# One transfer per expert: gate, up and down weights side by side in a diffusion trunk with 64 experts

## What is computed

```
def run_block(args):
    e, tok, wt = args
    xb = t_pad[tok]                                        # the tokens of expert e
    hb = jax.nn.silu(xb @ w_gate[e]) * (xb @ w_up[e])      # (tokens, 256)
    return (hb @ w_down[e]) * wt[:, None].astype(t.dtype)  # (tokens, 1024)
```

## Time and profile before

| | us |
|---|---|
| median of 3 runs (3128.2 to 3129.74) | 3129.06 |
| span of the profiled execution | 3130.5 |
| PE busy with matmuls | 2604.7 (83%) |
| PE weight loads | 1531.1 (49%) |
| DVE / ACT / POOL busy | 843.2 / 615.6 / 539.8 |
| hardware queue, share of 16 engines | 48.1%, 558.02 MB |
| software queue, share of 16 engines | 3.0%, 31.52 MB |

### The profile page before, as it was taken

The page is one execution under the profiler, slowest core; times in us unless marked ns, Lnnn a source line. Parts: engine busy times, 40 slices in busy tenths (PEclk is TensorE's granted clock), DMA queues, the critical chain, the costliest instruction groups (busy, mean ns, idle before and its releaser), DMA issues. The chain is left out here.

```text
span 3130.5 us, 33956 instructions
## 1 busy us (share of the span) xinstructions
PE 2604.7 (83%) x12570; PEld 1531.1 (49%) x12570; DVE 843.2 (27%) x1610; ACT 615.6 (20%) x1211; POOL 539.8 (17%) x502
## 2 busy tenths in 40 slices
PE   5998987889999996888888649789999878888882
PEld 1444556545556544555445334554544445455551
DVE  2443228144200035111111141714300241111113
ACT  2333210124300011111111122004300111111111
POOL 0000002036300001222222120105500022122222
PEclk8968998989999997999999879899999989999996
DMA  9564111002021323999999542101033369999992
GB/s 316 217 234 163 68 34 74 18 6 52 1 61 40 118 110 131 389 396 392 386 381 377 217 148 81 61 18 43 15 81 99 128 269 391 385 380 381 383 395 111
DMA packets 206864, 590.73 MB, mean 189 GB/s; under 512 B 47464, under 2 KB 104851, under 8 KB 156468
## 3 DMA queue, kind: packets, MB, share of 16 engines
q1 hardware_dynamic: 183828, 558.02, 48.1%
q0 software_dynamic: 22944, 31.52, 3.0%
HBM read 584.06 MB, written 51.51 MB: 203 GB/s over the span
## 5 line engine op out<-in xcount | busy, mean ns | idle before, releaser
L1920 PE MATMUL ps<-wgu,moe_xt 128*64 128x256 f32 x4096 | 508.9, 404 | 164.9 <-DMA wd<-in_w_down_e 162.6
L1920 PEld LDWEIGHTS ps<-wgu,moe_xt 128*64 128x64 f32 x4096 | 340.2, 145 | 291.6 <-issue 183.1
L1502 PE MATMUL ps<-u,w_merge 128*128 128x512 f32 (+1 forms) x768 | 282.0, 525 | 3.7 <-DVEq L1519 3.7
L2007 POOL DMA_INDIRECT rows_out<-moe_y,table x128 | 118.3, 924 | 818.5 <-DVE moe_y L2066 797.4
L1928 PE MATMUL ps<-wd,moe_ht 128*64 128x512 f32 x1024 | 247.8, 605 | 1.5 <-DVE moe_ht L2108 1.5
L2102 DVE TENSOR_TENSOR moe_h<-ps,moe_sg 64x256 f32<-64x256 f32 x128 | 54.5, 426 | 628.8 <-ACT moe_sg L2085 628.8
L812 PE MATMUL ps<-u,w_hy 128*128 128x512 f32 (+1 forms) x576 | 209.4, 521 | 5.8 <-PEq L125 5.8
L1502 PEld LDWEIGHTS ps<-u,w_merge 128*128 128x128 f32 x768 | 146.8, 191 | 134.9 <-issue 123.8
L2085 ACT ACTIVATE moe_sg<-ps 64x256 f32<-64x256 f32 x128 | 48.2, 376 | 638.5 <-PE ps L1920 638.5
L1259 POOL TENSOR_SCALAR attn_p<-attn_p,attn_rs 128x768 f32<-128x768 f32 (+1 forms) x80 | 155.1, 1947 | 81.6 <-DVE attn_rs L1428 81.2
L2066 DVE COPY moe_y<-ps 64x512 f32<-64x512 f32 x128 | 88.7, 693 | 265.4 <-PE ps L1928 265.4
(11 more groups left out here) (313 smaller groups left out, 3090.4 us busy)
## 6 DMA issues: line engine op xcount, KB each, us to landing
wgu<-in_w_gate_e SPq DMA_DIRECT2D x128, 1024.0 KB, 7.9
wgu<-in_w_up_e SPq DMA_DIRECT2D x128, 1024.0 KB, 10.6
wd<-in_w_down_e SPq DMA_DIRECT2D x128, 1024.0 KB, 17.6
prep_w<-in_w_ada SPq DMA_DIRECT2D x24, 2048.0 KB, 15.0
w_merge<-in_w_in SPq DMA_DIRECT2D x32, 512.0 KB, 5.3
w_hy<-in_w_in SPq DMA_DIRECT2D x6, 2048.0 KB, 9.5
transfer<-prep_out POOLq DMA_DIRECT2D x10, 1024.0 KB, 6.8
h<-transfer SPq DMA_DIRECT2D x4, 2048.0 KB, 11.4
```

The costliest lines, as they stand in the source:

```text
L1502: last = nc.tensor.matmul(m.ps[:, bank, 0:n], w[:, b, w_at + c], z[:, c, at:at + n], start=c == 0, stop=c == kn - 1)
L1920: last = nc.tensor.matmul(ps[k * SLOTS:(k + 1) * SLOTS, 0:DE], xt[:, c], wgu[:, k, c], start=c == 0, stop=c == KC - 1)
L2007: nc.gpsimd.indirect_dma_start(out=dram["y"], out_offset=bass.IndirectOffsetOnAxis(ap=m.table[0:SLOTS, j:j + 1], axis=0), in_=y[:, j % 2], ...
```

## The change

The three weight arrays of an expert are laid side by side on the host: a new input `w_experts` of (2, 64, 128, 6144), in which each partition's row holds its 2048 numbers of gate, of up and of down, 24 KB in one piece. A ring slot is one tensor of 128 x 24 KB, with views for the gate and up part and for the down part. `load_expert` issues one DMA of 3 MB and 16 is added once to the semaphore, so PE waits for 16 per use in place of 48. The overflow stage is changed in the same way. The order on every engine, the ring of four and the moments at which a slot is refilled are as before.

```diff
-def load_expert(eng, a, l, e, wgu, wd, sem):
-
-    for k, name in enumerate(("w_gate_e", "w_up_e")):
-        eng.dma_start(wgu[:, k], a[name][l, bass.ds(e, 1)].rearrange("o (p c) n -> p (o c) n", p=P)).then_inc(sem, 16)
-    eng.dma_start(wd, a["w_down_e"][l, bass.ds(e, 1)].rearrange("o (p c) n -> p (o c) n", p=P)).then_inc(sem, 16)
+def load_expert(eng, a, l, e, w, sem):
+
+    eng.dma_start(w, a["w_experts"][l, bass.ds(e, 1)].rearrange("o p n -> p (o n)")).then_inc(sem, 16)
+
+
+GU = 2 * KC * DE
+
+
+def gate_up_part(w):
+
+    return w[:, 0:GU].rearrange("p (k c n) -> p k c n", k=2, c=KC)
+
+
+def down_part(w):
+
+    return w[:, GU:GU + 2 * D].rearrange("p (c n) -> p c n", c=2)
...
-    wgu, wd, loaded = ring
+    slots, loaded = ring
+    wgu, wd = [gate_up_part(w) for w in slots], [down_part(w) for w in slots]
...
-                    load_expert(sp, a, l, j, wgu[b], wd[b][:], loaded[b])
+                    load_expert(sp, a, l, j, slots[b][:], loaded[b])
...
-                wait(pe, loaded[b], r * 48 + 48)
+                wait(pe, loaded[b], r * 16 + 16)
...
-            ring[0].append(whole.enter_context(nc.sbuf_tensor(f"wgu{l}_{b}", [P, 2, KC, DE], F32, side=side)))
-            ring[1].append(whole.enter_context(nc.sbuf_tensor(f"wd{l}_{b}", [P, 2, D], F32, side=side)))
+            ring[0].append(whole.enter_context(nc.sbuf_tensor(f"w{l}_{b}", [P, GU + 2 * D], F32, side=side)))
...
-                load_expert(sp, a, l, b, ring[0][b], ring[1][b][:], ring[2][b])
+                load_expert(sp, a, l, b, ring[0][b][:], ring[1][b])
...
+    laid = {name: np.ascontiguousarray(inputs[name]) for name in NAMES if name not in EXPERT_NAMES}
+    laid["w_experts"] = np.concatenate([np.ascontiguousarray(inputs[name]).reshape(DEPTH, NE, P, -1) for name in EXPERT_NAMES], axis=3)
```

More of the change, by code:

```diff
@@ L2169, in overflow_stage @@
             "block_done"]
-    bufs = [("wgu", [P, 2, KC, DE]), ("wd", [P, 2, D]), ("xg", [SLOTS, D]), ("xt", [P, KC, SLOTS]), ("sg", [P, DE]),
+    bufs = [("w", [P, GU + 2 * D]), ("xg", [SLOTS, D]), ("xt", [P, KC, SLOTS]), ("sg", [P, DE]),
             ("h", [SLOTS, DE]), ("ht", [P, 2, SLOTS]), ("y", [SLOTS, D]), ("idx", [SLOTS, 1], I32), ("row", [SLOTS, 1], I32)]
@@ L2186, in body @@
                 sp.wait_ge(s["pe_done"], i * 4 + 4)
-                load_expert(sp, a, l, e, s["wgu"], s["wd"][:], s["w_in"])
+                load_expert(sp, a, l, e, s["w"][:], s["w_in"])
             blocks(sp, body)
@@ L2218, in body @@
                 strided_transposes(nc, m.ps[:, 0], s["xg"][:], KC, m.ident).then_inc(s["pe_done"], 1)
-                pe.wait_ge(s["w_in"], i * 48 + 48)
+                pe.wait_ge(s["w_in"], i * 16 + 16)
                 pe.wait_ge(s["x_evac"], i + 1)
-                gate_up(nc, m.ps[:, 1], s["xt"], s["wgu"]).then_inc(s["pe_done"], 1)
+                gate_up(nc, m.ps[:, 1], s["xt"], gate_up_part(s["w"])).then_inc(s["pe_done"], 1)
                 pe.wait_ge(s["h_done"], i + 1)
@@ L2225, in body @@
                 pe.wait_ge(s["ht_evac"], i + 1)
-                down_both(nc, m.ps[:, 3], s["ht"], s["wd"]).then_inc(s["pe_done"], 1)
+                down_both(nc, m.ps[:, 3], s["ht"], down_part(s["w"])).then_inc(s["pe_done"], 1)
             blocks(pe, body)
@@ L2264, in experts @@
         m.rows = rows
-        ring = [], [], [nc.alloc_semaphore(f"expert_in{l}_{b}") for b in range(RU)]
+        ring = [], [nc.alloc_semaphore(f"expert_in{l}_{b}") for b in range(RU)]
         def ring_buffer(b, side):
-            ring[0].append(whole.enter_context(nc.sbuf_tensor(f"wgu{l}_{b}", [P, 2, KC, DE], F32, side=side)))
-            ring[1].append(whole.enter_context(nc.sbuf_tensor(f"wd{l}_{b}", [P, 2, D], F32, side=side)))
+            ring[0].append(whole.enter_context(nc.sbuf_tensor(f"w{l}_{b}", [P, GU + 2 * D], F32, side=side)))
         def first_round(sp, of):
             for b in of:
-                load_expert(sp, a, l, b, ring[0][b], ring[1][b][:], ring[2][b])
+                load_expert(sp, a, l, b, ring[0][b][:], ring[1][b])
         picks = {name: whole.enter_context(nc.sbuf_tensor(f"pick_{name}{l}", shape, F32))
@@ L2320 @@
          "w_router_g", "b_router_g", "w_router_e", "b_router_e", "w_gate_e", "w_up_e", "w_down_e", "final_g"]
+EXPERT_NAMES = ["w_gate_e", "w_up_e", "w_down_e"]
 def kernel(**inputs):
@@ L2328 @@
     arrays, a, consts = {}, {}, {}
-    for name in NAMES:
-        arrays[f"in_{name}"] = np.ascontiguousarray(inputs[name])
+    laid = {name: np.ascontiguousarray(inputs[name]) for name in NAMES if name not in EXPERT_NAMES}
+    laid["w_experts"] = np.concatenate([np.ascontiguousarray(inputs[name]).reshape(DEPTH, NE, P, -1) for name in EXPERT_NAMES], axis=3)
+    for name in laid:
+        arrays[f"in_{name}"] = laid[name]
         a[name] = nc.dram_tensor(f"in_{name}", arrays[f"in_{name}"].shape, F32, kind="ExternalInput").ap()
```

## The result

The changed kernel takes 3215.47 us (median; 3208.13 to 3224.51, 4 runs) against 3128.63 us for the kernel before (3120.79 to 3129.74, 4 runs): a ratio of 1.028, with a 95% interval of 1.026 to 1.031. It is 87 us slower. The profiled execution has a span of 3206.3 us, 76 more than that of before.

The account below looks back on a forecast made before the run. The weights' DMA was taken as the bound in the expert stages; after the change late gathers would set the period, adding 57 us in layer 0 and 63 in layer 1 to the median 3129.06: 3249 us, range 3108 to 3310.

Parts of the forecast that it names:

- Sizes of packets: Expert weight loads: a 24 KB run stays uncut, giving 8 packets per engine and expert, each 1.0 us long.
- Issue, waits for weights, layout: SP issues one DMA instead of three, PE waits for one transfer: worth nothing; only SBUF strides differ, matmul prices stay.
- Small packets: Expert loads: three completion packets per engine and expert become one, 0.16 us less, DMA work 8.54 and 8.39 us.
- Bytes in longer packets: Expert weights: extra price per byte in 24 KB packets between 0 and 12% (0.9 us per expert), taken as 0.
- Turns: POOL's gather and scatter packets each wait a weights packet: turn 0.36 to 1.03 us, scatter lands 10.75, gather 14.7 us.
- The cycle: Late gather holds down matmuls, scatter, next gather: landing plus 5.9 us over two periods, 10.3 us; P 9.69 and 9.64.
- The sum: Both expert stages, 58 experts each: 57 us more in layer 0, 63 in layer 1, together +120 us.
- Long packets doing no harm: Rival, expert stages: gather stays under 11.5 us, 0.16 us saved per expert, 19 us less, 3110 us; chance 0.23.
- No difference: Rival, expert stages: slower gather (11 or 12 us) just eats its slack, or 2% dearer bytes cancel savings; 3129; chance 0.09.
- Dearer bytes: Rival, expert weights: bytes cost 12% more, weights alone need 9.4 us, +165 us, 3294 us; chance 0.08.
- A fixed cost for each transfer: Rival, expert loads: each transfer blocks the engines; one for three gives 6.87 us period, 203 us less, 2926; chance 0.02.
- Turns of a transfer's whole share of an engine: Rival, POOL's queue: a turn is a load's whole share, gather 17.7 us, 11.8 per expert, +371, 3500 us; chance 0.02.

## Why the prediction was right, and where it was off

**Sizes of packets: right.** A 24 KB run stayed whole: 4149 long packets for 32 experts.

**Issue, waits for weights, layout: right.** One transfer in place of three, with 8 KB packets, is within 0.2% of the kernel before.

**Small packets: wrong.** I divided the 0.83 us per expert that the traffic loses beside gathers and scatters by the number of small packets, and priced a completion at 0.08 us, 0.16 us less per expert and 19 us in all. Two of three completions gone gave nothing that can be measured, 24 more packets per engine and expert cost 0.004 us each, and two packets of a gather fewer gave 0.04 us each, half of my price. So one price for all small packets was wrong: in these runs the packets of the other queue cost something, the weights' own nearly nothing. Without gathers and scatters an expert's weights take 7.45 us in place of 8.5 to 8.7. The rows' own bytes are 5% of what is moved (6.03 of 115.16 MB); how the remaining loss arises where two queues alternate is not shown.

**Bytes in longer packets: bounds missed.** I set 0 to 12% and took 0. Weights alone cost 2% less. The row of 16 KB was one short load with its own start and end, as I wrote. I should have let the lower end go below zero.

**Turns: right in kind.** Shown from both sides: three kernels keep the 24 KB packets and change something else (an earlier gather, another order, fewer rows), and get back 71 to 80 us; five only shorten the packets (8 KB twice, 12, 16 and 8, 4 KB), and are at most 10 us above the kernel before. The scatter landed at 10.2 us (forecast 10.75). The gather landed at 10.6, forecast 14.7: this is the term of the sum that was mis-sized. I let every gather wait for five full turns behind its scatter, 5.15 us. On average it comes 10.6 + 1.23 - 10.2 = 1.6 us behind, and pair by pair a third come 2.8 to 4.8 us and two thirds less than 1 us behind. For half of those two thirds the weights' queue was partly empty, which I had put only into the period, by a mean share. For the other half it was full, so turns of one packet each don't describe every gather; the reason is open.

**The cycle: right in kind, two sizes off against each other.** Landing plus 5.9 us over two periods gives 8.3 us with the median landing of 10.6. That is under the weights' 8.54: by my own rule (a gather is free up to 11.5 us) the kernel would have lost nothing. I measure 9.30 (layer 0) and 9.21 us (layer 1), from these rows of gate and up matmuls, which answer to the earlier trace rows:

```profile
1264.67 3.67 PE L1920 MATMUL ps<-w,moe_xt 128*64 128x256 f32 x32
```

```profile
1803.96 3.67 PE L1920 MATMUL ps<-w,moe_xt 128*64 128x256 f32 x32
```

```profile
2604.54 4.02 PE L1920 MATMUL ps<-w,moe_xt 128*64 128x256 f32 x32
```

```profile
3138.58 3.67 PE L1920 MATMUL ps<-w,moe_xt 128*64 128x256 f32 x32
```

(1803.96 - 1264.67) / 58 = 9.30 and (3138.58 - 2604.54) / 58 = 9.21; I had 9.69 and 9.64. What lifts 8.3 to 9.3 can be read from the means of layer 0, where 44 of the 59 landings from expert 5 on are on record. The gather lands after 11.0 us on average, 0.4 over the median. The transposes start 1.3 us after the landing on average, because in the other bodies PE gets to an early gather late: landing times are uneven (8.2 to 14.6 us), and an early gather doesn't repay what a late one costs, as the bodies of 6.9 and 13.4 us show. And the path of 5.9 us is 6.4 on average, since it contains the down matmuls, which cost 0.54 us more per body at the low clock, 0.27 per period. Together (11.0 + 1.3 + 6.4) / 2 = 9.35 us. So the slack must be held against the late gathers and not against the median one. With the landing of 14.7 us put too long and the unevenness and the clock left out, the two errors partly cancel; that 3249 came near 3215 is in part luck. One wording of mine is loose: the gather is used two bodies after the transposes from which I counted, which is the next body after its issue; the cycle of two periods is right.

**The sum.** It is 34.4 us in layer 0 and 38.2 in layer 1 over the 58 experts each, where I had 57 and 63. In the first five bodies, where I had nothing, it is 6.6 and 5.5 us more: the weights aren't the bound there, but gathers are already late (two waits of 1.1 and 4.1 us before the transposes in layer 0). Together 84.7 us, forecast 120.

**The rivals.** Long packets doing no harm was wrong for the kernel as it is, right for 12 KB. No difference asked for a gather of 11 or 12 us; the median of 10.6 is even below that, and still 87 us were lost, for the reason just given. Dearer bytes are out: the early gather has the same bytes in the same packets and lacks 80 of the 87 us. A fixed cost for each transfer isn't seen where transfers follow each other: three and one come out the same. The Trainium skill, page DMA: Bandwidth & Descriptors, section Anatomy of one DMA, gives about 2 us for it, and gives it for one transfer issued by GpSimd; the weights are issued by SyncE. Turns of a transfer's whole share of an engine would have put the gather at 17.7 us, and the longest on record is 14.6. The Trainium skill's section Queues, rings and completion order on the same page describes arbitration by packets of some 9 to 17 descriptors, and a load has 8 rows and a completion on an engine; the measured landings don't agree with it.

## What to carry to other kernels

In this kernel the latency of the small transfers grew with the length of the packets in the other queue: the scatter landed after 6.0, 6.7, 7.7 and 10.2 us beside packets of 4, 8, 12 and 24 KB. So before making runs longer, count the packets of the small transfers that share the engines, follow who waits for them, and work out their slack, for the latest one and not for the median. Here some 4 us of slack hid 12 KB packets and didn't hide 24 KB ones. When the landing of a small transfer is the trouble, issue it earlier or move what doesn't need it ahead of the wait; both gave back 70 to 80 of 87 us without touching the transfer of the weights.

## What I had not expected of the hardware

A wait that moves changes which matmuls pay for the low clock. In the kernel before, the down matmuls of every body took 1.94 us, and gate and up, behind the wait, were sometimes slow, with the DMA engines full all the same. Afterwards the down matmuls took 3.68 us behind a wait of 4.6 us, inside the cycle that set the time.

The weights' packets are nearly free in number (0.004 us each between 4 and 8 KB) and 2% dearer per byte at 8 KB than at 24 KB, so there was little to win from longer ones: 17 us of some 3000, measured with the engines to themselves.

At 24 KB a gather lands either some 4 us or less than 1 us behind the scatter ahead of it, and the second happens with the weights' queue full as well as empty. Beside 8 KB packets it was 1.4 to 2.9 us behind in layer 0, without such a split.
